# Score matmuls of one head group: the second of each pair contracts over 64 rows instead of 128

## The reference

```
def gqa_blocks(q, k, v):
    scale = q.shape[-1] ** -0.5
    def blk(qb):
        s = jnp.einsum('bqgrd,bkgd->bgrqk', qb, k).astype(jnp.float32) * scale
        p = jax.nn.softmax(s, axis=-1).astype(v.dtype)
        return jnp.einsum('bgrqk,bkgd->bqgrd', p, v)
    return over_query_blocks(blk, q)
```

## Time and profile before

| | us |
|---|---|
| median of 3 runs | 3073.74 (3071.2 to 3077.83) |
| profiled execution, its own time | 3077.83 |
| its span | 3076.0 |
| PE busy | 2543.6 (83%) |
| DVE busy | 1330.3 (43%) |
| ACT busy | 941.1 (31%) |
| POOL busy | 387.1 (13%) |

### The profile page before, as it was taken

One profiled execution on the slowest core, in us unless ns is written; L12 is line 12 of the kernel. 1 busy time (PEld: TensorE's weight loads), 2 busy tenths in 40 slices (PEclk: granted clock), 3 DMA queues, 4 the chain that ended last, 5 costly groups with the idle time before them and its releaser, 6 DMA issues. The chain is left out here.

```text
span 3076.0 us, 33678 instructions
## 1 busy us (share of the span) xinstructions
PE 2543.6 (83%) x13152; PEld 1653.7 (54%) x13152; DVE 1330.3 (43%) x2498; ACT 941.1 (31%) x1962; POOL 387.1 (13%) x280
## 2 busy tenths in 40 slices
PE   4969688888988987878959696798889889878798
PEld 1645555565456754654426455555654657556543
DVE  3242653443545354661133425534434544545611
ACT  1131102443244254461011320024421443544610
POOL 1220551000100000001213105510001000000012
PEclk9979889998999987888969798899989999878799
DMA  5420100100000000001143201001000000000021
GB/s 192 168 103 23 45 1 14 43 1 12 30 28 1 10 1 2 29 28 70 60 163 140 103 23 45 1 14 43 1 12 30 28 1 10 1 2 29 28 76 62
DMA packets 71848, 128.41 MB, mean 42 GB/s; under 512 B 22882, under 2 KB 35554, under 8 KB 70052
## 3 DMA queue, kind: packets, MB, share of 16 engines
q1 hardware_dynamic: 71688, 126.23, 11.9%
HBM read 109.02 MB, written 21.92 MB: 43 GB/s over the span
## 5 line engine op out<-in xcount | busy, mean ns | idle before, releaser
L588 PE MATMUL psum<-arena 128*32 128x256 f32 (+8 forms) x8496 | 1779.7, 456 | 232.4 <-POOL arena L1933 53.0
L588 PEld LDWEIGHTS psum<-arena 128*32 128x32 f32 (+3 forms) x8496 | 1033.1, 164 | 905.4 <-issue 627.6
L592 PE MATMUL psum<-ident,arena 128*128 128x128 f32 (+1 forms) x2248 | 415.1, 313 | 234.9 <-ACT arena L1241 143.0
L592 PEld LDWEIGHTS psum<-ident,arena 128*128 128x128 f32 (+1 forms) x2248 | 287.6, 155 | 388.5 <-ACT arena L1241 175.6
L1689 DVE TENSOR_REDUCE st<-psum 128x1 f32<-128x1152 f32 (+1 forms) x288 | 354.0, 1236 | 298.0 <-PE psum L588 297.4
L1425 DVE TENSOR_TENSOR arena<-arena 128x64 f32<-128x64 f32 (+9 forms) x638 | 328.9, 559 | 171.7 <-ACT arena L1376 61.4
L1241 ACT COPY arena<-psum 128x512 f32<-128x512 f32 (+1 forms) x472 | 206.7, 438 | 474.1 <-PE psum L592 473.4
L1225 ACT ACTIVATE arena<-psum,st 128x1152 f32<-128x1152 f32 (+1 forms) x288 | 325.6, 1131 | 79.8 <-DVE st L1689 70.9
L588 PE MATMUL psum<-k_parts,q_parts 96*128 96x384 f32 (+2 forms) x1000 | 297.3, 396 | 24.2 <-ACT arena L1225 13.5
L1933 POOL TENSOR_TENSOR arena<-arena 128x512 f32<-128x512 f32 (+2 forms) x98 | 273.3, 2804 | 294.5 <-DVE arena L1505 131.2
L1933 POOL TENSOR_TENSOR st<-st,mhalf 128x1 f32<-128x1 f32 (+2 forms) x72 | 56.3, 782 | 1555.9 <-DVE st L1430 1555.9
(11 more groups left out here) (126 smaller groups left out, 1247.0 us busy)
## 6 DMA issues: line engine op xcount, KB each, us to landing
arena<-in_ada_w SPq DMA_DIRECT2D x12, 2048.0 KB, 8.6
arena<-in_w_in SPq DMA_DIRECT2D x10, 2048.0 KB, 7.8
arena<-out_xs SPq DMA_DIRECT2D x36, 512.0 KB, 5.1
out_xs<-arena SPq DMA_DIRECT2D x18, 512.0 KB, 2.6
arena<-in_w_out SPq DMA_DIRECT2D x4, 2048.0 KB, 8.0
out_xs<-in_x SPq DMA_DIRECT2D x1, 4608.0 KB, 17.3
spectrum_kept<-arena SPq DMA_DIRECT2D x2, 2304.0 KB, 6.9
arena<-spectrum_kept SPq DMA_DIRECT2D x2, 2304.0 KB, 8.4
```

The lines of the kernel that those rows point to most:

```text
L588: return nc.tensor.matmul(out, lhsT, rhs, start=start, stop=stop)
L592: return nc.tensor.transpose(out, src, ident[0:n, 0:n])
```

## The change

The second matmul of each pair reads 64 partitions of both operands. The zeros are no longer multiplied, so the two memsets on POOL and PE's wait for them go too.

```
-                                last = mm(out, q_parts[:, m, qs], k_parts[:, m - m % 2 + 1, ks], False, True)
+                                last = mm(out, q_parts[0:64, m, qs], k_parts[0:64, m - m % 2 + 1, ks], False, True)
...
-                    if grp == "gqa":
-                        pe.wait_ge(*S.all("low_half_cleared"))
...
-                for half in (1, 3):
-                    link(nc.gpsimd.memset(k_parts[64:128, half, :].bitcast(F32), 0.0), "low_half_cleared")
```

## The result

The changed kernel took 3150.38 us (median of 4 runs, 3149.74 to 3151.91) against 3075.78 for the kernel before, measured beside it: ratio 1.0245, 95% interval 1.0227 to 1.0263. That is 75 us slower. The forecast had the direction and missed the size, 16 us, by more than four times.

What follows compares the result with a forecast made beforehand. PE was taken to bound the kernel, busy 83% of the span. Blocks 5.5, first units 1.8 and end 0.9 made 8.2 us a layer, 16.4 for both, on the median of 3073.74: 3090 us, range 3073 to 3106.

Steps and rivals of the forecast that it cites:

- The memsets and the wait: Removing POOL's two memsets (2.38 us together) and PE's wait at the start of attention was worth 0.
- What 64 rows save: In gqa's score matmuls, fewer rows save 0, since a matmul's stream is its 384 columns.
- What a change of form costs: On PE, each switch between 128-row and 64-row matmuls was taken to cost 0.09 us.
- The upper end: Highest price of a switch on PE: next matmul starts when the previous ended, 0.34 instead of 0.18, 0.16 us more.
- The sum over a block: One attention block of four steps grows by 0.91 us, the rest going into PE's waits; six blocks make 5.5 a layer.
- d: The price in us of one switch of array form between neighbouring matmuls on PE, taken as 0.09.
- step 2: Second of a block's four steps; its first flip waits for ACT's copy behind the exponentials, +0.45 us.
- Rival B: Array empties before each switch, weights load in the open, 0.16 us each: 17.1 a layer, 3108 us; chance 0.11.
- The comparison with mla: Mla's attention has 0.53 us more scores a unit; its steps differ by +0.53, 0, +0.28 against computed +0.54, -0.09, +0.32.
- The first units and the end: Each layer's seven units before the blocks grow by 1.8 us, the units behind them by 0.9 together.
- The clock: Sign of a wrong forecast: granted clock under 1.00 in attention from more PE pauses, costing far more; no chance given.
- Rival A: No price: 64 rows behave like mla's 96, score starts stay 0.18 us apart, total stays 3074 us; chance 0.21.

Runs made afterwards that it cites:

- memset_kept: The changed kernel with the two memsets on POOL and PE's wait for them put back; 3154.64 us, ratio 1.0230 to the kernel before.
- all64: The kernel before with both matmuls of each pair on 64 rows, leaving out a product; 3103.77 us, ratio 1.0067.
- later64: The changed kernel with the first 7 units of each layer back at 128 rows, the other 29 at 64; 3125.03 us, ratio 1.0130 to the kernel before.
- fp32_cols64: The changed kernel with both matmuls in float32, the second cut into two of 128 rows by 64 columns; 3297.0 us against 3087.5, one execution.
- grouped64: The changed kernel with each unit's three 128-row matmuls first, then its three 64-row ones; 3092.87 us, ratio 1.0032 to the kernel before.
- rows96: The kernel before with the second matmul of each pair on 96 rows, memsets and wait kept; 3083.85 us, ratio 1.0002.
- zigzag64: The changed kernel with the middle piece's 64-row matmul first, four changes of form a unit instead of six; 3116.81 us, ratio 1.0098 to the kernel before.
- cols96: The changed kernel with both matmuls of a pair on 96 of a tile's 128 queries; 3135.16 us in one execution.
- first64: The kernel before with 64 rows for the second matmul only in the first 7 units of each layer; 3112.84 us, ratio 1.0081.

## Why the prediction was wrong, point by point

**The memsets and the wait, booked at 0**: nothing in the traces speaks against it, and memset_kept does not differ; its spread leaves 3 us open.

**What 64 rows save, booked at 0**: right. all64 has 1.31 us for six.

**What a change of form costs, "I take 0.09 for each change"**: this is the step that failed first. The rows I used measured one distance, from the last matmul of one form to the first of the next, and that distance is indeed 0.09 longer. But the next one is longer as well, by 0.10 with a load of 128 columns and about half of that with 64, since the load behind a change is no longer hidden. With a change at every matmul both halves fall on each distance: 0.18 + 0.09 + 0.10 = 0.37, as measured. The upper end I gave, 0.16, was below the truth too. The trace of before shows the second half, and I passed it by. It stands right behind the product of the earlier trace rows from which I read 0.12, and behind the change from the values to the flips:

```profile
110.30 1.12 PE L588 MATMUL psum<-arena 64*128 64x512 f32 x2
110.83 1.02 PE L588 MATMUL psum<-arena 64*128 64x512 f32 x2
...
884.85 0.44 PE L592 MATMUL psum<-ident,arena 128*128 128x128 f32 x2
```

The first two 64-row products start 0.53 apart (110.30 and 110.83), the second and the third 0.43 (1.02 less the last one's 0.59): 0.10 more behind the change. The first two flips start 0.17 apart (0.44 - 0.27), others 0.11.

**The sum over a block**: wrong in its second half, and by the size of d. At d = 0.09 the exponentials hold step 2; at 0.19 PE holds every step, each is scores, four flips, ACT's copy and the last flip one after the other, 2.56 + 6d = 3.68, as measured. The growth is 1.12 + 0.39 + 0.86 + 0.64 = 3.0 a block, of which the fourth is five changes less the slack of 0.31. Rival B's formula, 16d - 0.54, kept the loop of the exponentials beyond the point where it holds (about d = 0.10) and gives 2.5 at 0.19. The comparison with mla was sound, but it tested 0.53 a unit, not 1.1. Rival B's start of 3.5 does not fit the forecast's own rule either (twice a block's 2.0 is 4.0); that moves its 3108 by about 1 us.

**The first units and the end, booked at 1.8 and 0.9 a layer**: by the estimate above the first units cost 4.3 at full clock; later64 has 1.0 for the end, so 0.9 was near, but by luck: the same sum at a d of 0.19 would give 1.9. With the blocks' 18.1 the changes alone are 23.4 a layer, 47 us in all and 3121 on the median of 3073.74: outside the range of 3073 to 3106 even if the clock had stayed.

**The clock**: named among what would prove the forecast wrong, "which would cost far more than all of this", and given no chance. It fell in the first units of both layers, for some 34 us at half clock, and by the estimate above cost 13 us each, 26 in all; later64 shows that the long fall comes only where the first units are changed. I expected it to follow PE's pauses. all64 shows that it falls with half of the rows in use and no change inside a unit, fp32_cols64 that it stays with the pauses and all rows in use. But grouped64, with the same matmuls as the changed kernel and a third of its changes, had 0.93 and 0.87 against 0.58, hardly less than rows96 with its 0.93, and zigzag64 lies between them. So both the rows and the changes have a part in it. Why only the first units are open to it is not shown: they have no values between them, but the DMA queues also move 51 to 89 GB/s there against 1 or 2 in the blocks, and no run separates the two. What sets off the fall stays open.

So the account of the 77.9 us of span is: 36 in twelve blocks, 9 in the first units at full clock, 26 by the clock there, 2 in the ends at full clock, 3.5 by the clock there, which unchanged kernels can show too, and 2 elsewhere. Rival A ("no price") is out; B was nearest in mechanism, with the load in the open, at 3108.

The Trainium skill's page "TensorEngine Tiling (Array Packing)", section Key Properties, has it that changing the tiling mode drains the TensorE; for the 64-row form all of these runs agree in that each such change costs time, and rows96 shows that 96 rows are no such change. The page "TensorE: Matmul & The Clock Gate", section on what happens when a matmul is issued, says that the time of a weight load goes with the columns and not with the rows; the changed kernel agrees (0.18 for 64 rows and 0.19 for 128, of 128 columns each), and so does cols96 (0.16 for 96 columns).

## What to carry to other kernels

Fewer rows in a matmul save nothing on PE, but 64 rows beside full ones make a change of form; group matmuls of one form, and count the distance behind a change as well as the one at it. Zeros that fill a matmul up to its neighbour's form may be cheaper than leaving them out. When the price of a term doubles, follow the loops again: another one may hold. And before a difference of the clock is put down to a change, look how much of it the unchanged kernel shows in other executions.

## What the runs showed of the hardware that was not expected

- A change of form costs 0.19 us at 2.4 GHz in two parts: 0.09 at the change, and behind it 0.10 to 0.11 for a load of 128 columns (0.06 where a flip follows).
- With PE busy in 40.15 of 40.20 us the granted clock was 0.58, so here a full list of matmuls did not keep the clock up; all64 had 0.56 in 27 us.
- The fall differs from layer to layer in one execution (0.58 and 0.84 over the same seven units in first64 and in memset_kept), which moves the whole by 9 us.
